# Gate and up products of a decoder layer: three byte offsets instead of one for the moving operands in SBUF

## What is computed

```python
x = x + mix @ w_out
h2 = rmsnorm(x, norm_ffn_g)
x = x + (silu(h2 @ w_gate) * (h2 @ w_up)) @ w_down      # w_gate, w_up: 1024 x 2816
return rmsnorm(x, final_norm_g)
```

## Time and profile before

| | us |
|---|---|
| three runs | 2961.68, 2962.1, 2985.42 (median 2962.1) |
| the profiled execution | 2961.26 |
| its span, first to last instruction | 2959.2 |
| TensorE busy in the span | 2874.5 (97%) |
| VectorE busy | 1951.8 (66%) |
| ScalarE busy | 1588.1 (54%) |
| GpSimd busy | 912.9 (31%) |

### The profile page before, as it was taken

How to read it: one execution, slowest core, us unless ns; L and a number is a source line. 1 busy time by engine, 2 the same in 40 slices (tenths; PEclk the granted TensorE clock), 3 DMA queues, 4 the chain that set the end, 5 groups by cost and what they waited for, 6 DMA issues and landing times.

```text
span 2959.2 us, 51857 instructions
## 1 busy us (share of the span) xinstructions
PE 2874.5 (97%) x19000; PEld 2579.5 (87%) x19000; DVE 1951.8 (66%) x2944; ACT 1588.1 (54%) x2672; POOL 912.9 (31%) x1022
## 2 busy tenths in 40 slices
PE   7999999999999999999999999999999999999998
PEld 6888878777777999999889998998889998999886
DVE  6215520277766777778668777876658888887656
ACT  5122211267777878887545555554445555655444
POOL 1922221156665877777401222111000000001100
PEclk9999999999999999999999999999999999999999
DMA  5488987436652440402248999999746775799964
GB/s 201 128 210 216 220 235 173 129 88 147 164 119 58 107 101 15 115 25 70 95 140 276 324 319 261 303 285 314 207 133 220 247 247 182 219 331 304 284 193 160
DMA packets 303481, 559.47 MB, mean 189 GB/s; under 512 B 32288, under 2 KB 70304, under 8 KB 302112
## 3 DMA queue, kind: packets, MB, share of 16 engines
q1 hardware_dynamic: 262912, 463.12, 49.3%
q0 software_dynamic: 39072, 92.30, 16.3%
q10 hardware_dynamic: 1312, 1.64, 0.2%
HBM read 449.98 MB, written 197.13 MB: 219 GB/s over the span
## 4 chain that ended last, share of the span: by engine, by line
PE 60%; DVE 9%; POOL 5%; ACT 3%; issue 2%; DMA 1%; DVEq 0%; SPq 0%; ACTq 0%; POOLq 0%
PE f_ps L2431 27%; PE f_ps L2323 18%; PE h_o L998 6%; PE h_t L984 3%; PE h_z L720 2%; PE h_z L723 2%; POOL h_more L1282 2%; DVE h_negmax L1118 2%; POOL h_work L1282 2%; DVE h_more L1234 2%; DVE h_more L1150 2%; ACT h_work L1017 1%; ACT h_more L1017 1%; POOL h_srstd L1327 1%; DMA f_wraw<-sums_scratch 1%
## 5 line engine op out<-in xcount | busy, mean ns | idle before, releaser
L1810 ACT ACTIVATE f_whi<-f_wraw 128x512 fp32r<-128x512 f32 x834 | 520.9, 627 | 399.4 <-PE f_ps L2431 252.7
L1817 DVE TENSOR_TENSOR f_wlo<-f_wraw,f_whi 128x512 fp32r<-128x512 f32 x834 | 574.8, 690 | 230.1 <-ACT f_whi L1810 228.3
L2431 PE MATMUL f_ps<-f_hi_s,f_whi 128*128 128x256 f32 x1408 | 392.0, 278 | 5.0 <-DVE f_up L2164 5.0
L2431 PE MATMUL f_ps<-f_hi_s,f_wlo 128*128 128x256 f32 x1408 | 391.1, 278 | 0.0
L2431 PE MATMUL f_ps<-f_lo_s,f_whi 128*128 128x256 f32 x1408 | 391.0, 278 | 0.0
L1322 POOL TENSOR_TENSOR h_work<-h_work,h_more 128x1024 f32<-128x1024 f32 (+3 forms) x192 | 302.2, 1586 | 110.4 <-DVE h_more L1234 97.6
L2431 PE MATMUL f_ps<-f_hi_a,f_whi 128*128 128x256 f32 x1056 | 293.5, 278 | 0.9 <-DVE f_second L2164 0.9
L2431 PE MATMUL f_ps<-f_hi_a,f_wlo 128*128 128x256 f32 x1056 | 293.3, 278 | 0.0
L2431 PE MATMUL f_ps<-f_lo_a,f_whi 128*128 128x256 f32 x1056 | 293.3, 278 | 0.0
L2431 PEld LDWEIGHTS f_ps<-f_hi_s,f_whi 128*128 128x128 f32 x1408 | 265.3, 188 | 6.8 <-DVE f_wlo L1817 4.1
L2431 PEld LDWEIGHTS f_ps<-f_lo_s,f_whi 128*128 128x128 f32 x1408 | 265.3, 188 | 0.0
(11 more groups left out here) (199 smaller groups left out, 6856.9 us busy)
## 6 DMA issues: line engine op xcount, KB each, us to landing
f_wraw<-in_w_stream SPq DMA_DIRECT2D x394, 256.0 KB, 4.5
f_wraw<-sums_scratch SPq DMA_DIRECT2D x352, 256.0 KB, 4.7
sums_scratch<-in_w_stream POOLq DMA_DIRECT2D x132, 256.0 KB, 5.2
act_scratch<-f_act SPq DMA_DIRECT2D x88, 256.0 KB, 4.2
combined_acts<-f_act SPq DMA_DIRECT2D x88, 256.0 KB, 5.2
f_wraw<-down_sums SPq DMA_DIRECT2D x88, 256.0 KB, 2.7
f_piece<-combined_acts SPq DMA_DIRECT2D x88, 256.0 KB, 2.9
down_sums<-in_w_stream POOLq DMA_DIRECT2D x66, 256.0 KB, 6.6
```

Source lines behind the costliest of these rows:

```text
L1810: act.activation(w_hi[ring][:], w_raw[ring][:], ACT.Copy).then_inc(S["hi_split"], 1)
L1817: dve.tensor_tensor(w_lo[ring][:], w_raw[ring][:], w_hi[ring][:].bitcast(F32), ALU.subtract).then_inc(S["lo_split"], 1)
L2431: mm = pe.matmul(outs[i], w[ring][:, col], a[name][:, c, :], start=(c == 0 and m == 0), stop=(c == 3 and m == 2))
```

## The change

SHIFT becomes a table by side: s2 and a22 begin 160 bytes past the grid, a11, s1 and a12 192, s3 and s4 224. In the order of products the shifts are 192, 160, 192, 224, 192, 160, 224 and then 192 again: no two neighbours are alike. The sides are also placed in the order of the table (s2, a22, a11, s1, a12, s3, s4) instead of that of OPERANDS, so that the shifts rise with the address and no side overlaps the next. The order of the products, every instruction, its size and its waits stay as they are.

```diff
-SHIFT = 192
+SHIFT = {"s2": 160, "a22": 160, "a11": 192, "s1": 192, "a12": 192, "s3": 224, "s4": 224}
...
-    home = {name: operands + 2 * row * i + SHIFT for i, name in enumerate(OPERANDS)}
+    home = {name: operands + 2 * row * i + SHIFT[name] for i, name in enumerate(SHIFT)}
     F["side_hi"] = {name: at("hi_" + name, [P, 4, SIDE], home[name], F32R) for name in OPERANDS}
     F["side_lo"] = {name: at("lo_" + name, [P, 4, SIDE], home[name] + row, F32R) for name in OPERANDS}
```

## The result

| | us |
|---|---|
| kernel before, median of 22 runs | 2971.91 (2961.68 to 2987.33) |
| changed kernel, median of 22 runs | 2986.93 (2977.57 to 2996.51) |
| ratio, with its 95% interval | 1.0038 (1.0024 to 1.0051) |
| the profiled execution of the changed kernel | 2989.33 (span 2987.4) |

The kernel became slower by 0.4%. That is under the 1% that I called measurable, yet the interval excludes no change. The forecast was 2953 us with a range up to 2984; the median lies above it. The three runs of before that the prediction had gave a median of 2962.1, 10 us under that of all 22, so the absolute number also holds a shift of the base.

A forecast was written before the change was run, and what follows sets the result against it. TensorE's matmul stream was taken to bound the gate blocks. From 2961.3 us, 11.2 less for the slow pace and 1 more for switches gave 2951; 1 us for slow block starts and 1 for weight waits made 2953, range 2949 to 2984.

The forecast's parts named there:

- Part 1: Gate block matmuls: 2545 run at the slow pace, 4.4 ns each, so 11.2 us could be gained if all went fast.
- The even sample of stalls: Gate blocks before the change: of 14 stalls that break the stream, 6 were followed by the fast pace, 8 by the slow.
- Two paces, 113.3 and 117.8: Gate blocks: identical matmuls start 113.3 or 117.8 ns apart, 4.4 ns between the two, changing only at stalls.
- Part 3: Matmuls on sides at 160 and 224: taken to run at the floor of 113.3 ns, with 0.12 us as upper end.
- A switch shakes the stream out of the slow pace: Gate blocks, likeliest case: changing side frees the stream and each side runs at 113.3 ns; 2950 to 2957 us, chance 0.40.
- redraw rival: Gate blocks: pace drawn anew at each of 616 switches, or no net effect; 2957 to 2972 us, chance 0.31.
- Part 2: 616 switches between sides in the gate blocks: nothing to 2.7 us in all, 1 us taken.
- Part 4: Writers of the sides, 28 on ACT and 44 on DVE: costed at nothing, 5 us if DVE had no spare time.
- part 5: New order in memory: out projection buffers overlap four other sides, but are read out before; cost nothing.
- What would show it wrong: Gate blocks: paces changing in mid-product, or a shift's own pace above 118 ns; elsewhere lengths were to keep within 1 us.
- The third pace: Rival: loads and columns at 160 or 224 collide, 121 ns on four sides, +26 us; 2987 to 3006 us, chance 0.06.
- The slower one: Rival: switches throw all 7392 gate matmuls to 117.8 ns, 2982 to 2985 us; mostly slow, 2972 to 2985, chance 0.21.

## Why the prediction was wrong

- **That PE's stream sets the gate blocks, 1 ns per matmul being 7.4 us**: right. 25 us of pace are 3.4 ns on each of 7392 matmuls.
- **Part 1, 11.2 us to be had from the slow pace**: right for the profile that it was read from (11.6), but four profiles with all sides at 192 hold 7 on average. The even sample of stalls (6 fast, 8 slow) is 7 and 7 if the last product of block 3 is counted as the fast one that it is.
- **Two paces, 113.3 and 117.8, that change only at stalls** with all sides at one shift: right, in three more profiles with all sides at 192. The floor of 113.3 held too: no stretch beat it.
- **Part 3, the pace at 160 and 224: this step failed.** I took the floor because the two shifts are nearer to 192 than to 0. They measured 117.5 to 118.7 and 118.3. Nearness says nothing, since the effect repeats: with 64, 192 and 448 fast at times and 96, 128, 160, 224 and 256 never, the fast pace looks like one with a period of 128 bytes, in which 160 and 224 are each 32 bytes off. The slow paces don't repeat so soon (120.0 at 0 and 256, 118.7 at 128 and 384). The upper bound that I had kept, 0.12, was nearer the truth than the floor. Four sides of seven thereby lost the fast pace for good: 4224 x some 5 ns are 21 us against a stream that is all fast. a11 and a12, slow behind 224, are another 2112 x 4.5 = 9.5, and with 1 for s1 that makes the 32 us.
- **"A switch shakes the stream out of the slow pace"**: the second step that failed. A switch of side does act on the phase, but not by shaking it loose or by chance, as the redraw rival had it: a product at 160 turns it over and one at 224 leaves it slow, without exception where no stall is near. 0 and 128 left it fast in each of four slow entries, 32 in six of nine. The changed kernel has the one shift that always leaves it slow ahead of a11 and a12.
- **Part 2, the cost of a switch**: 1 us taken, 2.7 as the bound. The entry of s1 takes 0.36 us for three distances (2364.86 to 2365.22) against 0.34 at its steady pace, some 20 ns to the rounding of the view, so it is a few slow distances and not one. That is under 2 us over the 88 tiles; at the other switches both sides are slow and nothing can be told apart.
- **Part 4 and part 5, the writers of the sides and the order in memory, at nothing**: right; DVE's writer at L2135 takes 1223 ns after the change and 1224 before, and the order alone left the blocks at 852.4. The buffers of the out projection don't overlap four other sides than before, as part 5 says, but three of the same and a22 in place of s3.
- **What would show it wrong**: both signs came. The pace of 160 lies above 118, and paces change in mid-product, in s1 after three distances. Outside the gate blocks the length did not keep to 1 us either: in the first pair of profiles 11.5 us more ahead of them and 3.4 less behind block 1.
- **Two rivals share the truth.** The third pace, at 0.06, had the mechanism of the four sides: a distance that belongs to s2 and a22 (118.8) and to s3 and s4 (118.3) alone. Its size was too large, 121 for 118.5; with that its sum is 4224 x 3.6 = 15 us instead of 26. The slower one, at 0.21, mostly slow at 2982 to 2985, had a11 and a12 right, which a switch leaves slow, but named the switch as such, by likeness to the start of a block; the kernel with 160 and 192 and those with a11 alone elsewhere show switches that leave the fast pace. That its time lies 2 us from the median is luck: it added 21 to 24 us where the medians differ by 15, from a base that stood 10 us too low. The range left the spread of the base out, although the third of the runs, 2985.42, hinted at it.
- **The page's rule on independent read ports** ("SBUF — State Buffer", "Who interferes with whom", of the Trainium skill): it says PE never waits on anyone. The runs don't agree with it as far as PE's own two reads go: moving only the distance between them changed the matmul from 113.3 to 120.0 ns. That the two reads collide is still an inference from the distance; no view shows the reads.

## What to carry to other kernels

When two profiles of the same code, or two blocks of one profile, show different distances between identical matmuls, look at where the streamed operand begins against the stationary one before looking for a wait. Sweep that distance a shift per block in one kernel, since shifts near a good one may be bad, and read the steady distance and not the total, which hides a stream that is drawn fast or slow. Don't vary a placement that has been found good to break a pattern: a neighbour at a bad distance costs its own pace and can set the pace of those behind it.

## What the runs showed of the hardware

- A stream of weight loads (128 columns of float32r) and matmuls of 256 columns runs at 113.3 to 120.0 ns per matmul at the full clock, depending on the distance in bytes, modulo 512, between the beginnings of the two operands (64, 192 or 448: 113.3 or 117.7; 160: 117.5 or 118.7; 224: 118.3; 128 or 384: 118.7; 0, 96 or 256: 120.0).
- At 192 both paces are stable over more than a thousand matmuls. A stall, or one product of 12 matmuls at another distance, can change them.
- Streams of 512 columns feel the distance as well, less: in the kernel with the weights moved by 64 bytes against the activations, which are the stationary operand there, 70.00/305 = 229.5 ns per matmul against 70.00/308 = 227.3 in the same window before. The mean over the whole trace, waits left out, is 228.9 against 226.8.

```profile
2830.00:2900.00 70.00, 70.00 (x307) 1.00 0.60 192
```

```profile
2830.00:2900.00 70.00, 70.00 (x310) 1.00 0.61 194
```
